# Seven quarter products instead of eight in the second products of layer 1's MLP and of the two feed-forward blocks

## The chip, the cores and the metric

The kernel runs on one core of one Trainium2 chip. Its time is the device time of one launch in microseconds (us): before the change 2538.02 us, the median of three runs (2536.36 to 2540.02). In the rows below PE is TensorE (PEld its weight loads), DVE is VectorE, ACT is ScalarE, POOL is GpSimd and SP the engine that issues most DMAs. Differences of up to 0.2% (5 us) are what a measurement of this kernel can't tell from none.

## The reference

512 tokens of width 1024 in float32 go through two layers (a short convolution, then a recurrent mixer, each with an MLP) and a block with two gated feed-forward parts around attention. Only these lines bear on the change:

```python
# layer i, width 1024 -> 4096 -> 1024
x = x + gt2[:, None, :] * (jnp.square(jax.nn.relu(h @ mlp_w1[i])) @ mlp_w2[i])
# feed-forward block, width 1024 -> 2816 -> 1024, twice
def swiglu(h, w_gate, w_up, w_down):
    return (jax.nn.silu(h @ w_gate) * (h @ w_up)) @ w_down
x = x + 0.5 * swiglu(rmsnorm(x, ffn1_norm[l]), ...)
x = x + 0.5 * swiglu(rmsnorm(x, ffn2_norm[l]), ...)
```

## The kernel before, in words

Activations lie transposed: a tile has 128 channels on the partitions and the 512 tokens along the row. A product `h @ w` is cut into blocks of 128 output channels and chunks k of 128 input channels. float32 is kept by splitting: a value is its rounded high part plus the rest, and of the four products of parts three are made. So each (block, k) costs three matmuls of 128x128 by 512 tokens: high weights by high input (line 624), high weights by low input (628), low weights by high input (630).

`PROJ` lists the products in order with the number of blocks and chunks; `pieces()` cuts their weights into pieces of up to eight 128x128 tiles (one DMA of 512 KB each into `raw_`, four buffers). Kind "m" has a piece of eight chunks of one block; kinds "e", "f" and "g" begin with 8, 6 or 4 blocks at once, chunk by chunk (so that these blocks all end within one piece), and go on as "m". For every piece ACT rounds the high part (line 1218, `WHs`, three buffers), then DVE subtracts it (line 1780, `WLs`). Both engines run through their own programs in order, and `AHEAD = 2`: in the step of piece u they first make the weights of piece u+2, and after that take what piece u has ended (`evac`). Nothing reorders this at run time. ACT can't round piece v before TensorE has used piece v-3.

In layer 1's MLP `mw1_1a` (16 blocks) and `mw1_1b` (16 blocks) are the first products. ACT takes a block out of PSUM with ReLU into `tmp` (line 1329) and writes the high part of its square to `HM` (1331), DVE squares `tmp` (1973) and writes the low part (1975). `mw2_1a` and `mw2_1b` (8 blocks of 16 chunks) read `HM`; their `evac` on DVE adds a block times its gate to X (1839). In the feed-forward blocks `f1gu` and `f2gu` (44 blocks, gate and up in turn, 22 pairs j) are the first products: DVE scales a block into one of eight buffers `pr` (2315), ACT takes the sigmoid (1588), POOL multiplies (2545), DVE makes the product h3 (2303), ACT its high part (1579), DVE the low part (2305), both in `HID`. `f1d` and `f2d` (8 blocks of 22 chunks) read `HID`. The last block of `f2d` is made in two token halves (lines 1184 to 1187), so that the last norm and the output can begin on the first half. The two products with a memory of 256 tokens (`wkv`, inputs `MNs`) already use matmuls of 256 columns at lines 624 to 630.

Of the kernel before, what the change touches and what calls it, by code (L numbers as in the profile page):

```python
# [71 lines left out]


# [74 lines left out]
class Banks:  # L148
# [204 lines left out]
def memory_order():  # L353
# [10 lines left out]
    for n in range(16):  # L364
# [8 lines left out]
            "w_o": ("back", "m", "m1"), "mw2_1a": ("m", "m2", None), "mw2_1b": ("m2", "fg", "fg"),  # L373
            "f1d": ("f1", "at", "at"), "w_out": ("at", "xa", "xa"), "wo": ("xa", "f2", "f2"),
            "f2d": ("f2", "end", "end")}
GATE = {"cw_out": (0, 2), "mw2_0a": (0, 5), "mw2_0b": (0, 5), "w_o": (1, 2), "mw2_1a": (1, 5), "mw2_1b": (1, 5),
        "f1d": 0.5, "w_out": 1.0, "wo": 1.0, "f2d": 0.5}

GAINS = {"mw2_1b": "fg1", "f1d": "mix_norm", "wo": "ffn2_norm"}


def build(nc, D, out):
    ctx = ExitStack()
    with ctx:
# [7 lines left out]
        names += ["w_lo", "v_const", "v_mod", "v_norm", "v_in", "v_evac", "v_mix", "v_scan", "v_attn"]  # L392
# [26 lines left out]
        oka = sb("oka", [128, 8])  # L419

# [16 lines left out]
        HID = at_("HID", WK + 32768, [128, 2, 22, 512], F32R)  # L437
# [48 lines left out]
        pr = [tmp_[:, i] for i in range(4)] + [T2[:, 0], T2[:, 1], GH[:, 0], GH[:, 1]]  # L486
# [51 lines left out]
        hid = lambda k: (HID[:, 0, k], HID[:, 1, k])  # L538
        xm = lambda i: (lambda k: (MX[i][0][:, k], MX[i][1][:, k]))
# [8 lines left out]
        def gate(name, m):  # L548
            g = GATE[name]
            return md(*g, m) if isinstance(g, tuple) else g  # L550

# [14 lines left out]
        def pe_program(pe, on):  # L566
# [85 lines left out]

            def turn(o, x, events, sem, cols=4):
# [31 lines left out]
            def raw(u):  # L685
                on.wait_ge(*S.at("raw", u))
                return raw_[:, u % NRAW]
# [268 lines left out]
            dense("mw1_1a", h, lambda k: ("HL", "m1", k))  # L956
            dense("mw2_1a", hm, lambda k: ("mlo", "mw1_1a", k))
            dense("mw1_1b", h, lambda k: ("HL", "m1", k))
            dense("mw2_1b", hm, lambda k: ("mlo", "mw1_1b", k))
# [21 lines left out]
            def ffn(n, tag):  # L981
                dense("f%dgu" % n, h, lambda k: ("HL", tag, k), after=norms_within if tag == "fg" else norm_within(tag))
                dense("f%dd" % n, hid, lambda k: ("hlo", n, k), part=slice(0, (None, -3)[n - 1]))
# [164 lines left out]
            def ending():  # L1148

                k0, m = [0, 8, 16], 7  # L1150
# [20 lines left out]
                for hf in range(2):  # L1171
                    o = bank("f2d", m, hf)
                    for j, (u, mms, _) in enumerate(list(steps("f2d"))[-3:]):
                        s = SLOT[u]
                        if hf == 1 and j == 1:
                            factors(0)
                        if hf == 1 and j == 2:
# [1567 lines left out]
```

## Time and profile before

| | us or share |
|---|---|
| median of 3 runs | 2538.02 |
| the profiled execution, its own time | 2542.36 |
| its span | 2540.6 |
| PE busy | 2490.3 (98%) of the span |
| DVE busy | 1329.9 (52%) |
| ACT busy | 908.6 (36%) |
| POOL busy | 201.8 (8%) |
| PE on the chain that ended last | 92% |
| mean granted clock of TensorE | 0.988 |

A matmul's duration in the profile holds its way through the array, and the next one starts before it ends; what a stream of them costs is read from start to start. A row that merges several instructions gives their number after x.

### The profile page before, as it was taken

Reading aid. Unit: us, or ns where it says so; the run is one execution under the profiler, and the core shown is the slowest. Engines: PE = TensorE matmul, PEld = TensorE weight load, DVE = VectorE, ACT = ScalarE, POOL = GpSimd, SP = SyncE. Lnnn points to the kernel's source line nnn. Section 1 sums busy time; section 2 is a strip of 40 time slices with the busy share of each in tenths; the row PEclk is TensorE's granted clock in tenths of the full one; section 3 lists DMA queues with packets and bytes.
Section 4 is the critical chain, followed back from the end, with each engine's and each line's share of the span. In section 5 each row is a group of like instructions: output and inputs, shape, how many; then the busy total and the mean of one; then the engine's idle time right before and its main releaser. Section 6 shows DMA issues by size and latency. Waiting matters only on the chain.

```text
span 2540.6 us, 39183 instructions
## 1 busy us (share of the span) xinstructions
PE 2490.3 (98%) x16966; PEld 2050.9 (81%) x16966; DVE 1329.9 (52%) x1967; ACT 908.6 (36%) x1364; POOL 201.8 (8%) x176
## 2 busy tenths in 40 slices
PE   9999999999999999999999999999999999999998
PEld 7888888876787887888888888888668987888887
DVE  7865746647845446543444544432345745444433
ACT  4224323337633233431433322322256444322221
POOL 1000000000220000000000111000221000111100
PEclk9999999999999999999999999999999999999999
DMA  8563665622210003232222332333112422322232
GB/s 341 192 197 117 200 197 185 189 86 81 85 39 4 5 29 126 82 108 99 93 100 75 108 100 95 91 97 124 64 48 76 141 79 65 114 92 99 87 100 71
DMA packets 79725, 271.86 MB, mean 107 GB/s; under 512 B 8912, under 2 KB 11216, under 8 KB 79040
## 3 DMA queue, kind: packets, MB, share of 16 engines
q1 hardware_dynamic: 67696, 224.79, 26.9%
q0 software_dynamic: 11856, 44.55, 5.5%
q8 instruction: 134, 2.20, 0.3%
q14 instruction: 39, 0.32, 0.0%
HBM read 265.11 MB, written 4.19 MB: 106 GB/s over the span
## 4 chain that ended last, share of the span: by engine, by line
PE 92%; DVE 5%; ACT 2%; issue 1%; DMA 0%; SPq 0%; DVEq 0%; ACTq 0%
PE ps L624 26%; PE ps L630 22%; PE ps L628 22%; PE ps L640 3%; PE ps L643 3%; PE ps L655 1%; DVE WLs L1780 1%; PE ps L796 1%; PE ps L809 1%; DVE ada L1796 1%; PE ps L597 1%; PE ps L822 1%; PE ps L693 1%; PE ps L1119 1%; PE ps L1133 1%
## 5 line engine op out<-in xcount | busy, mean ns | idle before, releaser
L1780 DVE TENSOR_TENSOR WLs<-raw,WHs 128x1024 fp32r<-128x1024 f32 (+2 forms) x406 | 461.4, 1137 | 419.4 <-ACT WHs L1218 418.7
L624 PE MATMUL ps<-HH,WHs 128*128 128x512 f32 x1728 | 646.6, 400 | 3.7 <-DVE Pq L2332 2.1
L1218 ACT ACTIVATE WHs<-raw 128x1024 fp32r<-128x1024 f32 (+2 forms) x424 | 416.7, 984 | 550.7 <-PE ps L630 444.7
L630 PE MATMUL ps<-HH,WLs 128*128 128x512 f32 x1406 | 548.3, 390 | 1.2 <-DVE WLs L1780 1.2
L628 PE MATMUL ps<-HL,WHs 128*128 128x512 f32 x1406 | 547.7, 390 | 0.0
L624 PEld LDWEIGHTS ps<-HH,WHs 128*128 128x128 f32 x1728 | 324.9, 189 | 76.0 <-issue 11.2
L630 PEld LDWEIGHTS ps<-HH,WLs 128*128 128x128 f32 x1406 | 263.9, 188 | 57.2 <-DVE WLs L1780 1.6
L628 PEld LDWEIGHTS ps<-HL,WHs 128*128 128x128 f32 x1406 | 264.4, 188 | 53.7 <-issue 2.2
L624 PE MATMUL ps<-HM,WHs 128*128 128x512 f32 x576 | 224.1, 389 | 0.0
L628 PE MATMUL ps<-HM,WHs 128*128 128x512 f32 x576 | 224.1, 389 | 0.0
L630 PE MATMUL ps<-HM,WLs 128*128 128x512 f32 x576 | 224.1, 389 | 0.0
L2545 POOL TENSOR_TENSOR tmp<-tmp,sqa 128x512 f32<-128x512 f32 x24 | 41.2, 1721 | 1099.0 <-ACT sqa L1588 1099.0
L630 PE MATMUL ps<-HID,WLs 128*128 128x512 f32 x330 | 128.4, 389 | 0.0
L624 PE MATMUL ps<-HID,WHs 128*128 128x512 f32 x330 | 128.4, 389 | 0.0
L628 PE MATMUL ps<-HID,WHs 128*128 128x512 f32 x330 | 128.4, 389 | 0.0
L630 PEld LDWEIGHTS ps<-HM,WLs 128*128 128x128 f32 x576 | 108.1, 188 | 22.5
L628 PEld LDWEIGHTS ps<-HM,WHs 128*128 128x128 f32 x576 | 108.1, 188 | 22.4
L624 PEld LDWEIGHTS ps<-HM,WHs 128*128 128x128 f32 x576 | 108.1, 188 | 22.4
L1796 DVE CUSTOM_DVE_ANT_0 ada<-ada,cbc 128x1024 f32<-128x1024 f32 x96 | 116.9, 1217 | 0.1
L1264 ACT ACTIVATE sqa<-X 128x512 f32<-128x512 f32 x63 | 39.8, 632 | 203.2 <-DVE X L1839 203.2
L1973 DVE TENSOR_TENSOR tmp<-tmp 128x512 f32<-128x512 f32 x64 | 44.2, 690 | 102.7 <-ACT HM L1331 102.6
L1329 ACT ACTIVATE tmp<-ps 128x512 f32<-128x512 f32 x64 | 38.0, 593 | 150.0 <-PE ps L630 150.0
(419 smaller groups left out, 3449.0 us busy)
## 6 DMA issues: line engine op xcount, KB each, us to landing
ada<-in_adaw POOLq DMA_DIRECT2D x80, 512.0 KB, 4.5
raw<-in_f1gu_m SPq DMA_DIRECT2D x38, 512.0 KB, 3.3
raw<-in_f2gu_m SPq DMA_DIRECT2D x38, 512.0 KB, 3.2
raw<-in_mw_0b SPq DMA_DIRECT2D x32, 512.0 KB, 3.5
raw<-in_mw_1b SPq DMA_DIRECT2D x32, 512.0 KB, 3.5
raw<-in_w_in_m SPq DMA_DIRECT2D x18, 512.0 KB, 3.3
ada<-in_adaw SPq DMA_DIRECT2D x16, 512.0 KB, 15.7
raw<-in_cw_in_m SPq DMA_DIRECT2D x16, 512.0 KB, 3.4
```

The costliest lines, as they stand in the source:

```text
L624: pe.matmul(o[m], WHs[:, s, w], hi, start=k == 0, stop=False)
L628: pe.matmul(o[m], WHs[:, s, w], lo, start=False, stop=False)
L630: t = pe.matmul(o[m], WLs[:, s, w], hi, start=False, stop=k == DEPTH_K[name] - 1)
L640: pe.matmul(o[m], WLs[:, s, 128 * c:128 * c + 128], x(k)[0], start=False, stop=False)
L643: t = pe.matmul(o[m], WHs[:, s, 128 * c:128 * c + 128], x(k)[1], start=False, stop=False)
L1218: act.activation(WHs[:, SLOT[v], 0:n], raw_[:, v % NRAW, 0:n], ACT.Copy).then_inc(*S.up("w_hi", ("hi", v)))
L1264: act.activation(sqt[f % 2][:, 0:n], src, ACT.Square).then_inc(*S.up("a_norm", ("sq", tag, f)))
L1329: act.activation(tmp_[:, m % 4], taken(name, m), ACT.Relu).then_inc(*S.up("a_evac", ("relu", name, m), ("free", name, m)))
L1780: dve.tensor_tensor(WLs[:, s, 0:n], raw_[:, v % NRAW, 0:n], WHs[:, s, 0:n].bitcast(F32), SUB).then_inc(*S.up("w_lo", ("lo", v)))
L1796: dve.tensor_tensor_reduce(tile, tile, cbc, 1.0, 0.0, MUL, ADD, mod[:, u:u + 1]).then_inc(*S.up("v_mod", ("dot", u)))
L1973: dve.tensor_tensor(x, x, x, MUL).then_inc(*S.up("v_evac", ("t2", name, m)))
L2545: pool.tensor_tensor(a_, a_, sqt[j % 2], MUL).then_inc(*S.up("g_ffn", ("ga", n, j)))
```

## The change

The input of a second product is grouped in pairs of chunks, its output in pairs of blocks, and the tokens in two halves (`early`, `late`). A quad of two blocks by two chunks by two halves took eight products of 128x128 by 256 tokens (in the form of four of 512); by Strassen's scheme in Winograd's form it takes seven, of sums of weight tiles and of sums of inputs. This is done for `mw2_1a` and `mw2_1b` (now 12 chunks each, `mw2_1c` takes the last 8 as before), and for the first 12 of the 22 chunks of `f1d` and `f2d` (`_a`; `_b` takes the last 10 as before). The first products are cut alike; `mw1_1a` is now 12 blocks, 8 of them at once, then 4.

```diff
-        ("mw1_1a", "e", 16, 8), ("mw2_1a", "m", 8, 16), ("mw1_1b", "m", 16, 8), ("mw2_1b", "m", 8, 16),
-        ("f1gu", "f", 44, 8), ("f1d", "m", 8, 22),
+        ("mw1_1a", "e", 12, 8), ("mw2_1a", "s", 8, 12), ("mw1_1b", "m", 12, 8), ("mw2_1b", "s", 8, 12),
+        ("mw1_1c", "m", 8, 8), ("mw2_1c", "m", 8, 8),
+        ("f1gu_a", "f", 24, 8), ("f1d_a", "s", 8, 12), ("f1gu_b", "m", 20, 8), ("f1d_b", "m", 8, 10),
...
-        ("f2gu", "f", 44, 8), ("f2d", "m", 8, 22)]
+        ("f2gu_a", "f", 24, 8), ("f2d_a", "s", 8, 12), ("f2gu_b", "m", 20, 8), ("f2d_b", "m", 8, 10)]
+BANK = [1, 2, 1, 3, 1, 2, 1]
+BEFORE = {2: 0, 4: 2, 5: 1, 6: 4}
+INPUT_GROUP = [0, 2, 1, 3, 1, 2, 3]
+SUMMED = (1, 2, 4, 6)
...
+            def fast(name):
+                src = name.replace("mw2", "mw1")
+                for a in range(BLOCKS[name] // 2):
+                    o = {}
+                    for i in range(7):
+                        u, b, g = FIRST[name] + 7 * a + i, BANK[i], INPUT_GROUP[i]
+                        if b not in o:
+                            o[b] = bank(name, a, b, hold=True)[:, 0:256]
+                        else:
+                            on.wait_ge(*S.at("drawn", name, a, BEFORE[i]))
...
+                        for k in range(n):
+                            w = slice(128 * k, 128 * k + 128)
+                            on.wait_ge(*S.at("ch", src, k, g))
+                            pe.matmul(o[b], WHs[:, s, w], HT[:, 0, k, x], start=k == 0 and i not in BEFORE, stop=False,
+                                      skip_group_check=i in BEFORE)
+                            on.wait_ge(*S.at("cl", src, k, g))
+                            pe.matmul(o[b], WHs[:, s, w], HT[:, 1, k, x], start=False, stop=False, skip_group_check=i in BEFORE)
+                            on.wait_ge(*S.at("lo", u))
+                            t = pe.matmul(o[b], WLs[:, s, w], HT[:, 0, k, x], start=False, stop=k == n - 1, skip_group_check=i in BEFORE)
...
+            def draw(name, a, i):
...
+                dve.scalar_tensor_tensor(out=x, in0=taken(name, a, b)[:, 0:256], scalar=gate(name, m) if sign > 0 else minus_gate(name, m),
+                                         in1=x, op0=MUL, op1=ADD).then_inc(*S.up("v_evac", *events))
...
+            def combinations(src, k, even, odd, t1, t2, t3, t4):
+                dve.tensor_tensor(t3, odd[:, late], even[:, late], SUB).then_inc(*S.up("v_in", ("T3", src, k)))
+                on.wait_ge(*S.at("T1", src, k))
+                dve.scalar_tensor_tensor(out=t2, in0=t1, scalar=-1.0, in1=odd[:, late], op0=MUL, op1=SUB).then_inc(*S.up("v_in", ("T2", src, k)))
+                on.wait_ge(*S.at("T2", src, k))
+                dve.scalar_tensor_tensor(out=t4, in0=t2, scalar=-1.0, in1=odd[:, early], op0=MUL, op1=SUB).then_inc(*S.up("v_in", ("T4", src, k)))
...
+            def hidden_fast(name):
+                def finish(m):
+                    k, x = m // 2, tmp_[:, m % 4]
+                    if m % 2 == 0:
+                        low(name, k, 0, x[:, early])
+                    else:
+                        low(name, k, 2, T2[:, 1])
+                        low(name, k, 1, T2[:, 0])
+                        low(name, k, 3, x)
```

`fast` is TensorE's part; `draw` (after each of the seven products), `combinations` (128x256 each) and `hidden_fast` are DVE's. The weights of one pair of output blocks come in four DMAs of 384 KB, the four quarters, each of six 128x128 tiles (768 wide); four of the seven pieces are sums of quarters, which DVE makes in `sum_quarters`, called one piece before the weights' low part. Each of the seven pieces is 6 chunks by 3 matmuls. Per pair of input blocks the input has seven 256-token groups, written as one of 256 (group 0) and three of 512 (groups 1 to 3), each with a high part by ACT (`high`, line 1466) and a low part by DVE (`low`, line 2219). The buffers `pr` go from four pairs to three, since `GH` now holds a weight sum. In `f2d_b` the last block in token halves has 10 chunks instead of 22, and the small matmuls of the last norm go in after its chunks 4 and 7 of the second half.

On DVE, in `mw1_1a`, this is what is done when the first 8 blocks have ended (tmp: the block; HM or HT: high and low parts; T_78: the input sums; WLs: low weights). Before, from the fifth of these blocks on:

```order
945 L1973 TENSOR_TENSOR tmp<-tmp 128x512
946 L1975 TENSOR_TENSOR HM<-tmp,HM 128x512
947 L1973 TENSOR_TENSOR tmp<-tmp 128x512
948 L1975 TENSOR_TENSOR HM<-tmp,HM 128x512
949 L1973 TENSOR_TENSOR tmp<-tmp 128x512
950 L1975 TENSOR_TENSOR HM<-tmp,HM 128x512
951 L1973 TENSOR_TENSOR tmp<-tmp 128x512
952 L1975 TENSOR_TENSOR HM<-tmp,HM 128x512
953 L1780 TENSOR_TENSOR WLs<-raw,WHs 128x1024
```

Now, one pair of blocks out of the four:

```order
945 L2234 TENSOR_TENSOR tmp<-tmp 128x512
946 L2219 TENSOR_TENSOR HT<-T_78,HT 128x512 x2
947 L2219 TENSOR_TENSOR HT<-tmp,HT 128x512
948 L2208 TENSOR_TENSOR T_78<-tmp 128x256
949 L2234 TENSOR_TENSOR tmp<-tmp 128x512
950 L2219 TENSOR_TENSOR HT<-tmp,HT 128x256
951 L2211 TENSOR_TENSOR T_78<-tmp 128x256
952 L2213 SCALAR_TENSOR_TENSOR T_78<-T_78,tmp 128x256
953 L2215 SCALAR_TENSOR_TENSOR T_78<-T_78,tmp 128x256
```

Two blocks took 4 instructions and take 10 now; the low weights that followed all eight blocks still follow all eight.

Where `f1gu` (now its first part, `f1gu_a`) ends and the second product begins, DVE's last pair and the next weights read like this before:

```order
1212 L2315 TENSOR_TENSOR tmp<-ps,sqa 128x512
1213 L2303 TENSOR_TENSOR tmp<-tmp 128x512
1214 L2305 TENSOR_TENSOR HID<-tmp,HID 128x512
1215 L2303 TENSOR_TENSOR tmp<-tmp 128x512
1216 L2305 TENSOR_TENSOR HID<-tmp,HID 128x512
1217 L1780 TENSOR_TENSOR WLs<-raw,WHs 128x768
```

and now (T_78 and tmp: `pr`; GH and wsum: sums of weight quarters; the last but one is the draw of the first of the seven products):

```order
1369 L2606 TENSOR_TENSOR T_78<-ps,sqa 128x512
1370 L2580 TENSOR_TENSOR tmp<-tmp 128x512
1371 L2208 TENSOR_TENSOR tmp<-tmp 128x256
1372 L2219 TENSOR_TENSOR HT<-tmp,HT 128x256
1373 L2580 TENSOR_TENSOR T_78<-T_78 128x512
1374 L2211 TENSOR_TENSOR T_78<-T_78,tmp 128x256
1375 L2213 SCALAR_TENSOR_TENSOR tmp<-tmp,T_78 128x256
1376 L2215 SCALAR_TENSOR_TENSOR T_78<-tmp,T_78 128x256
1377 L2219 TENSOR_TENSOR HT<-T_78,HT 128x512
1378 L2219 TENSOR_TENSOR HT<-tmp,HT 128x512
1379 L2219 TENSOR_TENSOR HT<-T_78,HT 128x512
1380 L1955 TENSOR_TENSOR WLs<-GH,WHs 128x768
1381 L2044 SCALAR_TENSOR_TENSOR X<-ps,X 128x256
```

The last pair's work has grown from 5 instructions to 11, and the low weights of piece 2 and the draw of product 0, which product 2 waits for, stand behind them.

## Rows read from the trace of the kernel before

**Rows 1.** The page, chain that ended last: shares of the span by engine.
```profile
PE 92%; DVE 5%; ACT 2%; issue 1%; DMA 0%; SPq 0%; DVEq 0%; ACTq 0%
```
**Rows 2.** Busy time by stretch: us, PE, PEld, DVE, ACT, POOL, granted clock, DMA.
```profile
1070.00:1375.00 305.00, 305.00 (x1347) 252.65 (x1347) 132.26 (x154) 104.11 (x137) 0.00 (x0) 1.00 0.29 96
1396.00:1723.00 327.00, 327.00 (x1444) 270.79 (x1444) 151.20 (x177) 96.34 (x121) 38.25 (x22) 1.00 0.31 98
```
**Rows 3.** Chain of waits, first steps of mw1_1a, 512 columns: start, us, what.
```profile
1029.64 1.82 PE ps L640 x8
...
1062.29 1.81 PE ps L640 x8
```
**Rows 4.** Timeline, wkv, 256 columns: start, us, engine, line, what.
```profile
2009.77 0.28 PE L630 MATMUL ps<-MNs,WLs 128*128 128x256 f32 x1
...
2013.97 0.28 PE L628 MATMUL ps<-MNs,WHs 128*128 128x256 f32 x1
```
**Rows 5.** Timeline of TensorE, first matmul of block 8 of mw1_1a.
```profile
1071.19 0.39 PE L624 MATMUL ps<-HH,WHs 128*128 128x512 f32 x1
```
**Rows 6.** Timeline of DVE, the eight blocks of mw1_1a that end together.
```profile
1068.25 0.69 DVE L1973 TENSOR_TENSOR tmp<-tmp 128x512 f32<-128x512 f32 x1
1068.98 0.69 DVE L1975 TENSOR_TENSOR HM<-tmp,HM 128x512 fp32r<-128x512 f32 x1
1069.59 0.68 DVE L1973 TENSOR_TENSOR tmp<-tmp 128x512 f32<-128x512 f32 x1
...
1078.88 1.22 DVE L1780 TENSOR_TENSOR WLs<-raw,WHs 128x1024 fp32r<-128x1024 f32 x1
```
**Rows 7.** Timeline of ACT there, the ReLU of block 9 once it has ended.
```profile
1082.27 0.60 ACT L1329 ACTIVATE tmp<-ps 128x512 f32<-128x512 f32 x1 [2.95 <-PE ps L630]
```
**Rows 8.** Groups by shape: 768-wide weights (mean ns after the bar); 256-wide (min/median/max ns).
```profile
L1780 DVE TENSOR_TENSOR WLs<-raw,WHs 128x768 fp32r<-128x768 f32 x40 | 38.3, 959 | 51.2 <-ACT WHs L1218 50.9
L1218 ACT ACTIVATE WHs<-raw 128x768 fp32r<-128x768 f32 x40 | 33.4, 835 | 37.4 <-PE ps L643 27.9 <-PE ps L630 9.5
...
L1687 ACT ACTIVATE MNs<-MEM x8: 417/418/419, 1980.3 to 1996.2; 128x256 fp32r<-128x256 f32 x8
L2430 DVE TENSOR_TENSOR MNs<-MEM,MNs x8: 424/424/426, 1980.8 to 1996.7; 128x256 fp32r<-128x256 f32 x8
```
**Rows 9.** Timelines of DVE and ACT in f1gu, one pair j.
```profile
1436.60 0.69 DVE L2315 TENSOR_TENSOR tmp<-ps,sqa 128x512 f32<-128x512 f32 x1 [3.06 <-PE ps L630]
1437.21 0.68 DVE L2303 TENSOR_TENSOR GH<-GH 128x512 f32<-128x512 f32 x1
1438.59 0.69 DVE L2305 TENSOR_TENSOR HID<-GH,HID 128x512 fp32r<-128x512 f32 x1 [0.70 <-ACT HID L1579]
...
1437.92 0.63 ACT L1579 ACTIVATE HID<-GH 128x512 fp32r<-128x512 f32 x1 [5.12 <-DVE GH L2303]
```
**Rows 10.** Ending: first half block's start (first and last start), second norm spread, DVE.
```profile
L1184 PE MATMUL ps<-HID,WHs x44: 278/283/364, 2512.7 to 2529.5; 128*128 128x256 f32 x44
...
2527.29 0.60 PE L1168 MATMUL ps<-ident,r 128*128 128x128 f32 x4
...
2531.07 0.41 DVE L2503 SCALAR_TENSOR_TENSOR X<-ps,X 128x256 f32<-128x256 f32 x1
```
**Rows 11.** The clock after gaps: timeline, chain, and stretches (clock third from the end).
```profile
1022.10 1.05 PE L588 MATMUL ps<-ones,sqa 128*128 128x1 f32 x8 [0.72 <-ACT sqa L1264]
1023.88 3.62 PE L597 MATMUL ps<-ident,r 128*128 128x128 f32 x16 [0.73 <-DVE r L1811]
...
1392.58 1.78 PE ps L597 x16
...
953.99 0.50 PE L919 MATMUL ps<-GHs,WHs 128*128 128x512 f32 x1 [1.65 <-DVE WLs L1780]
...
1023.90:1027.30 3.40, 3.40 (x16) 3.30 (x16) 0.75 (x1) 0.62 (x1) 0.00 (x0) 0.52 0.00 0
952.00:956.00 4.00, 2.35 (x49) 1.60 (x49) 1.23 (x1) 1.66 (x3) 0.00 (x0) 1.00 0.00 0
```

More of the change, by code:

```diff
@@ L70, with load_read @@
 POOLED = range(FIRST["w_in"] + 8, LAST["w_in"] + 1)
+LOADS = []
+RAW = {}
+for _u, _p in enumerate(WANT):
+    if _p[1] != "s":
+        RAW[_u] = len(LOADS)
+        LOADS.append((_u, None))
+    elif _p[3] == 0:
+        for _q in range(4):
+            RAW[_u, _q] = len(LOADS)
+            LOADS.append((_u, _q))
+HALT_LOAD = RAW[HALT]
+def load_read(load):
+    v, q = LOADS[load]
+    if q is not None:
+        return [("lo", v), ("lo", v + 4), ("lo", v + 5), ("sum", v + 6)][q]
+    return ("used" if v in WHOLE else "lo", v)
 TOKENS = [slice(0, 256), slice(256, 512)]
@@ L955, in pe_program @@
             norm("m1")
[L956 to L959, printed above, removed]
+            for part in "ab":
+                dense("mw1_1" + part, h, lambda k: ("HL", "m1", k))
+                fast("mw2_1" + part)
+            dense("mw1_1c", h, lambda k: ("HL", "m1", k))
+            if KIND["mw2_1c"] == "s":
+                fast("mw2_1c")
+            else:
+                dense("mw2_1c", hm, lambda k: ("mlo", "mw1_1c", k))
             def norm_within(tag):
@@ L1344, in within @@
                         shifted("m%d" % layer, layer, 3, i + 3)
-                for half in "ab":
-                    dense("mw1_%d%s" % (layer, half), hidden("mw1_%d%s" % (layer, half)), within if half == "a" else None)
-                    dense("mw2_%d%s" % (layer, half), residual("mw2_%d%s" % (layer, half)))
+                for part in MLP[layer]:
+                    one, two = "mw1_%d%s" % (layer, part), "mw2_%d%s" % (layer, part)
+                    dense(one, (hidden_fast if KIND[two] == "s" else hidden)(one), within if part == "a" else None)
+                    dense(two, residual(two))
             mlp(0)
@@ L1994, in within @@
                         after(i)
-                for half in "ab":
-                    dense("mw1_%d%s" % (layer, half), hidden("mw1_%d%s" % (layer, half)), within if half == "a" else after)
-                    dense("mw2_%d%s" % (layer, half), residual("mw2_%d%s" % (layer, half)), after)
+                for part in MLP[layer]:
+                    one, two = "mw1_%d%s" % (layer, part), "mw2_%d%s" % (layer, part)
+                    dense(one, (hidden_fast if KIND[two] == "s" else hidden)(one), within if part == "a" else after)
+                    dense(two, residual(two), after)
             mlp(0, ada_step)
@@ L2560, in weights @@
             def weights(first, last):
-                for v in range(first, last):
+                for r in range(first, last):
+                    v, q = LOADS[r]
                     name, kind, a, k, n = WANT[v]
```

374 lines of the change are left out of this document (283 added, 91 removed), and 3 rows, old and new, of the table RESIDUAL.

## The prediction, written before the changed kernel ran

> **What bounds the kernel now.** The chain that ended last is the first view: 92% of it is TensorE [rows 1]. The second is busy time by stretch: from 1070 to 1375 us (layer 1's MLP) and from 1396 to 1723 us (first feed-forward block) TensorE is busy in every microsecond at full clock, while DVE has work for 132 of 305 and 151 of 327 us [rows 2]. So the kernel is a stream of matmuls, and the change has to be judged by the length of that stream and by new gaps in it. The third view is the timeline, read from start to start. At 512 columns 18 groups of 8 matmuls take 1062.29 - 1029.64 = 32.65 us, or 0.2267 us each [rows 3]. At 256 columns 35 steps take 2013.97 - 2009.77 = 4.20 us, or 0.120 us each [rows 4]. Half the columns cost 53% of the time, not 50%.
>
> **The stream.** A product cut to 12 chunks was 8 x 12 x 3 = 288 matmuls of 512 columns, 65.3 us. As quads it is 4 x 7 x 6 x 3 = 504 matmuls of 256 columns, 60.5 us. One eighth of the arithmetic (8.2 us) shrinks to 4.8 us. Four products give 19.2 us. The ending takes part of this back and gives another part. Before, its last block in halves began at 2512.7 and the second norm spread at 2527.29, 14.6 us later; the last X update waits for the outputs of the first half and starts 3.8 us after the spread [rows 10], and that part stays. Now the first half has 30 matmuls (3.6 us), the second 24 up to the spread (2.9 us), and the small norm matmuls about 0.7: 7.2 us. The whole of f2d was 7 x 66 x 0.2267 + 14.6 = 119.3 us up to the spread and is now 60.5 + 7 x 30 x 0.2267 + 7.2 = 115.3. So f2d gives 4.0 us instead of 4.8, and all four give 3 x 4.8 + 4.0 = **18.5 us** (rounded).
>
> The Trainium skill, page "TensorE: Matmul & The Clock Gate", section "Back-to-back issue gap", gives a fixed cost of only 2.5 ns beside the columns. By it a matmul would take 109 ns at 256 columns and 216 ns at 512, and an estimate from that page alone is a gain of 28 us. The rows have 120 and 227 ns for this kernel's operands, so they decide, and the page's rule gets no chance of its own.
>
> **Inside a quad nothing new should wait.** A piece of weights now lasts 18 x 0.120 = 2.16 us on TensorE. DVE gives each piece one 768-wide low part (0.96 us, and about 0.88 to the next start, since starts lie 0.08 closer than durations: 0.61 for 0.69 in [rows 6]), one draw of 256 from PSUM (0.41 [rows 10]), and for four of seven a 768-wide sum (0.88). That is at most 2.2 us in four steps and 1.3 in three, 12.6 us of the quad's 15.1. ACT gives 0.84 [rows 8]. The low part of piece u+2 is wanted two pieces later, so a step that is 0.05 late shows nowhere. Cost taken: 0. If the cover is gone, it would cost what DVE exceeds 15.1 us by, sixteen times.
>
> **The burst in mw1_1a.** Eight blocks end together. DVE took 16 instructions for them, from 1068.25 to 1078.88, and then made the low weights of block 10 [rows 6]. Block 8 starts at 1071.19 [rows 5], blocks last 24 x 0.2267 = 5.44, so block 10 starts at 1082.07 and wants its low weights at 1082.5, with 2.4 us to spare. Now each pair of blocks costs DVE: two squares (0.61 each), a 256-wide low part (0.42 by [rows 8], 0.34 to the next), T1, T3, T2, T4 (0.34, 0.34, then 0.46 where the next waits for it, 0.34), three 512-wide low parts (0.61 each), and 0.2 of waiting for ACT's first high part. That is 5.1 us; the first pair lacks the low parts before it. 1.1 + 2.1 + 3 x 5.1 = 18.4, so the low weights of block 10 start at 1086.7 and are there at 1087.95. TensorE waits **5.4 us**, in two parts (ACT's high part is late too, at about 1085.5). The three-operand 256-wide forms on SBUF are not in the trace; between the 0.34 taken and the 0.69 of a 512-wide one this wait is 4 to 9 us; I take the form of equal width. Queued behind it: the low weights of block 11 and the work of blocks 8 and 9, which still end before block 11 starts.
>
> **The four entries to a quad product.** Before, a second product wanted its last input only at chunk 15 or 21, over 10 us after it began. Now piece 0 reads all six chunk pairs in 2.2 us, piece 1 another group of each, and piece 2 waits for its weights and for the draw of product 0, which both stand behind the last input pair in DVE's order. With T the end of the last block, for mw1_1b: ReLU T+0.20 to 0.80 [rows 7], square to 1.55, low part of group 0 at 1.5, T3, T2, T4 done 3.05, high part of group 2 by ACT to 3.75 and of groups 1 and 3 to 4.85, high weights of piece 2 to 5.6, low weights 5.65 to 6.6, draw to 6.95. Piece 2 starts at T+7.05 instead of 4.32: **2.7 us**. In mw1_1a DVE comes late from the burst, with two blocks' work and two weight sums in 10 us: by the same steps 3.7 us. In the feed-forward blocks the chain is scale, h3 of pair 10, h3 of pair 11 (0.61 to 0.71 apart [rows 9]), then as above: T4 is done at T+4.25, the low weights at 7.9, the draw at 8.35, and piece 2 starts at 8.45: 4.1 us each, 8.2 for two. Sum of the entries **14.7 us**, the largest wait in each being some 2.4 us ahead of piece 2. The bursts of six blocks at the start of f1gu_a and f2gu_a gain four 256-wide steps and two more low parts, some 3 us of DVE; the low weights behind them have two blocks (10.9 us) of room, as in mw1_1a, with 6 blocks instead of 8 in front. I take 0.3 us each (0 to 3). New waits together: 5.4 + 14.7 + 0.6 = **20.7 us**. Gates, buffers (three pairs of `pr` where j lasts 10.9 us and its work about 5) and DMAs (4 of 384 KB in 15.1 us) come at nothing: the matmuls hide them.
>
> **The clock.** Two gaps of 0.72 and 0.73 us with little work between them were followed by a stretch at a granted clock of 0.52, in which 16 transposes took 3.62 us instead of 1.78 [rows 11], so 1.7 us was lost. A lone gap of 1.65 us left the clock at 1.00 [rows 11]. The burst (over 5 us idle with a few matmuls in it) and the two feed-forward entries (some 3.7 us idle in 5) should each bring such a fall; the two MLP entries (2.4 us in one piece) are open. Cost 3 x 1.7 = **5.1 us**, from 0 to 5 x 1.84 = 9.2.
>
> **The sum.** -18.5 + 20.7 + 5.1 = +7.3 us on the profiled execution (own time 2542.36, span 2540.6). That execution was 4.3 us over the median of the runs; the difference is taken over to the median: 2538.0 + 7.3 = **2545.3 us**. Its own range, from the bounds above, is 2540 to 2553.
>
> **The rivals.**
> - *The clock holds.* Against it stand the double gap of [rows 11], for it the lone gap. Then -18.5 + 20.7 = +2.2: 2540 us, no change that can be told.
> - *The entries are shorter than drawn*, so the change is faster. The place is piece 2 of the first quad of each product, the price the 2.4 us before it, four times. It decides once all new waits are below 13.4 us (18.5 less the 0.2% of a measurement). That needs ACT's high parts and DVE's low parts to overlap better than one after another in queue order: if each entry is 2 us shorter (the last input's three low parts no longer in front) and the burst 3.4 us, with one fall of the clock, it is -18.5 + 20.7 - 8 - 3.4 + 1.7 = -7.5: 2530.5 us. For it speaks that DVE is idle over half of these stretches [rows 2]; against it that the order is fixed and the idle time lies after, not before, the low weights.
> - *DVE becomes the bound inside the quads.* For it: four steps of seven hold 2.2 us of work against 2.16. Against: the quad has 2.5 us to spare. If each piece ran 0.15 us over (a wait for the previous result before each draw would do it), 112 pieces give 16.8 us: 2562 us.
> - *The seven products aren't cheaper at all*: it would need 0.13 us per matmul. The rows of 256 columns, with the same three forms and new weights for each matmul, exclude it, unless the column sums read worse; within the third rival.
>
> **Chances.** Forecast 0.50, clock holds 0.20, shorter entries 0.18, DVE as bound 0.12. Faster by over 0.2% (5 us, what a measurement of this kernel can tell; under 2532.9): the third case and a sliver of the second, 0.19. Within 0.2%: most of the case with the clock held and a sixth of the forecast, 0.25. Slower (over 2543.1): 0.56. The range that holds 8 of 10 is 2530 to 2557.
>
> **What would show it.** Matmuls of 256 columns 0.120 us apart inside quads, and no waits there: the stream is right. In mw1_1a a wait of 5 us for ACT's and DVE's weights ahead of block 10: the burst. Ahead of piece 2 of four products a gap of 2.4 us that ends with a draw, and 1 us before it for a low input part: the entries. A granted clock below 1 after the burst and in both feed-forward entries: the fall. The forecast is wrong if the waits of TensorE grow by less than 13 us, or if gaps recur in each quad.

## The result and the profile after

The changed kernel takes 2545.39 us (median of 14 runs, 2542.5 to 2549.83), the kernel before beside it 2537.94 (14 runs, 2535.47 to 2542.18). The ratio is 1.0027 with a 95% interval of 1.0019 to 1.0036: the change costs 7 us, or 4.8 to 9.1 us by the interval. Forecast were 2545.3 us.

The page of the changed kernel has these totals, its chain by engine and its quad matmuls (busy us, mean ns; idle before them and who ended it):

```profile
PE 2474.5 (97%) x17794; PEld 2073.4 (82%) x17794; DVE 1528.2 (60%) x2352; ACT 973.3 (38%) x1484; POOL 199.2 (8%) x176
PE 88%; DVE 6%; ACT 2%; issue 2%; SPq 1%; DMA 1%; POOL 0%; DVEq 0%; ACTq 0%
L758 PE MATMUL ps<-HT,WHs 128*128 128x256 f32 x672 | 192.3, 286 | 8.3 <-DVE X L2044 7.7
```

TensorE is busy 15.8 us less than before (2490.3) and waits more: its share of the chain falls from 92% [rows 1] to 88%, DVE's rises from 5% to 6%. The third line is new: 7.7 us of TensorE's waiting ends with a draw. The same two stretches as in [rows 2] (us, PE, PEld, DVE, ACT, POOL, granted clock, DMA):

```profile
1070.00:1375.00 305.00, 296.20 (x1757) 264.73 (x1756) 222.20 (x329) 132.33 (x191) 0.00 (x0) 0.98 0.29 94
1396.00:1723.00 327.00, 324.07 (x1661) 277.64 (x1660) 198.32 (x270) 111.00 (x150) 37.02 (x22) 1.00 0.30 95
```

Before, TensorE had no idle microsecond in either; now 8.8 and 2.9 us are idle, and in the first the clock isn't full. The view of waits between 1020 and 1400 us (total, times, longest) gives the releasers:

```profile
PE ps L758 <- DVE X L2044: 3.9, 2, 2.0
PE ps L713 <- ACT WHs L1348: 2.7, 1, 2.7
PE ps L719 <- DVE WLs L1955: 2.0, 1, 2.0
```

Stage by stage, from one first matmul to the next in the two traces, in us:

| stage | before | after | difference |
|---|---|---|---|
| layer 1's MLP (before from 1027.55, after from 1024.51) | 348.29 | 353.96 | +5.7 |
| first feed-forward block | 365.2 | 363.3 | -1.9 |
| what lies between | 424.8 | 424.7 | -0.1 |
| second feed-forward block to the end of the span | 374.7 | 377.0 | +2.3 |
| from mw1_1a's start to the end | 1513.0 | 1519.1 | +6.0 |

Ahead of mw1_1a, where nothing was changed, the profiled execution of the changed kernel happened to be 3.0 us shorter. So the two spans (2540.6 and 2543.6) differ by 3.0 only; the 1513.0 and 1519.1 us are the fair comparison, and their difference lies within the interval of the ratio.

### The profile page after: what moved, and what is told of

It is laid out like the page before. It is cut to its first block, busy times and chain, and to the rows that moved or that the text cites. A ratio compares the mean times of both kernels' runs of the same rounds, so it can differ in the third digit from the quotient of the medians.

```text
span 2543.6 us, 41536 instructions
## 1 busy us (share of the span) xinstructions
PE 2474.5 (97%) x17794; PEld 2073.4 (82%) x17794; DVE 1528.2 (60%) x2352; ACT 973.3 (38%) x1484; POOL 199.2 (8%) x176
## 4 chain that ended last, share of the span: by engine, by line
PE 88%; DVE 6%; ACT 2%; issue 2%; SPq 1%; DMA 1%; POOL 0%; DVEq 0%; ACTq 0%
PE ps L713 22%; PE ps L719 18%; PE ps L717 18%; PE ps L729 4%; PE ps L732 4%; PE ps L758 3%; PE ps L763 3%; PE ps L761 3%; PE ps L770 1%; DVE WLs L1955 1%; PE ps L911 1%; PE ps L924 1%; ACT WHs L1348 1%; SPq L2874 1%; DVE HT L2219 1%
## 5 line engine op out<-in xcount | busy, mean ns | idle before, releaser
L1955 DVE TENSOR_TENSOR WLs<-raw,WHs 128x1024 fp32r<-128x1024 f32 (+3 forms) x430 | 465.6, 1083 | 283.0 <-ACT WHs L1348 281.5
L1348 ACT ACTIVATE WHs<-raw 128x1024 fp32r<-128x1024 f32 (+3 forms) x448 | 421.6, 943 | 454.8 <-PE ps L719 259.6
L758 PE MATMUL ps<-HT,WHs 128*128 128x256 f32 x672 | 192.3, 286 | 8.3 <-DVE X L2044 7.7
L761 PE MATMUL ps<-HT,WHs 128*128 128x256 f32 x672 | 192.4, 286 | 1.0 <-DVE HT L2219 0.7
L763 PE MATMUL ps<-HT,WLs 128*128 128x256 f32 x672 | 191.6, 285 | 0.0
L713 PE MATMUL ps<-HM,WHs 128*128 128x512 f32 x384 | 149.4, 389 | 0.0
L717 PE MATMUL ps<-HM,WHs 128*128 128x512 f32 x384 | 149.4, 389 | 0.0
L719 PE MATMUL ps<-HM,WLs 128*128 128x512 f32 x384 | 149.4, 389 | 0.0
L758 PEld LDWEIGHTS ps<-HT,WHs 128*128 128x128 f32 x672 | 130.4, 194 | 10.0 <-DVE X L2044 8.6
L761 PEld LDWEIGHTS ps<-HT,WHs 128*128 128x128 f32 x672 | 130.3, 194 | 2.5 <-DVE HT L2219 2.2
L763 PEld LDWEIGHTS ps<-HT,WLs 128*128 128x128 f32 x672 | 130.4, 194 | 0.0
L2606 DVE TENSOR_TENSOR tmp<-ps,sqa 128x512 f32<-128x512 f32 x60 | 40.8, 689 | 105.5 <-PE ps L719 105.5
L713 PEld LDWEIGHTS ps<-HM,WHs 128*128 128x128 f32 x384 | 72.1, 188 | 15.1
```

Of the source, the lines that this page charges most:

```text
L713: pe.matmul(o[m], WHs[:, s, w], hi, start=k == 0, stop=False)
L717: pe.matmul(o[m], WHs[:, s, w], lo, start=False, stop=False)
L719: t = pe.matmul(o[m], WLs[:, s, w], hi, start=False, stop=k == DEPTH_K[name] - 1)
L758: pe.matmul(o[b], WHs[:, s, w], HT[:, 0, k, x], start=k == 0 and i not in BEFORE, stop=False, skip_group_check=i in BEFORE)
L761: pe.matmul(o[b], WHs[:, s, w], HT[:, 1, k, x], start=False, stop=False, skip_group_check=i in BEFORE)
L763: t = pe.matmul(o[b], WLs[:, s, w], HT[:, 0, k, x], start=False, stop=k == n - 1, skip_group_check=i in BEFORE)
```

## The experiments

The theory: the stream of matmuls did get 18.5 us shorter; three kinds of loss took it back and more, namely the burst in mw1_1a, the wait for a draw at each entry, and falls of TensorE's clock after these gaps. Rivals: the burst or the entries cost little; the clock isn't a cost of its own; the 256-column matmuls or DVE inside the quads ate the gain. Each ratio is to the kernel before on the same chip, so ratios can be set side by side and medians of different chips can't: the kernel before took 2537.2 us beside e1 to e4, 2540.13 beside e5 to e8 and 2538.75 beside e9 and e10. e8 rests on two runs, e4 on four, e10 on six, the others on ten or more. "From mw1_1a" is the time from its first matmul to the end of the span in the profiled execution (before 1513.0).

| kernel | median us | ratio, 95% interval | from mw1_1a |
|---|---|---|---|
| changed (first) | 2545.39 | 1.0027, 1.0019 to 1.0036 | 1519.1 |
| e1_four | 2537.2 | 0.9997, 0.9988 to 1.0006 | 1512.3 |
| e2_entry | 2536.88 | 1.0, 0.9991 to 1.0009 | 1513.7 |
| e3_both | 2531.57 | 0.9977, 0.9968 to 0.9986 | 1506.2 |
| e4_narrow | 2560.97 | 1.0091, 1.0077 to 1.0105 | 1534.4 |
| e5_fill | 2538.99 | 0.999, 0.998 to 1.0 | 1508.2 |
| e6_end | 2533.69 | 0.9971, 0.996 to 0.9982 | 1504.8 |
| e7_slack256 | 2548.95 | 1.0031, 1.002 to 1.0041 | 1519.3 |
| e8_slack512 | 2563.26 | 1.0086, 1.006 to 1.0112 | 1531.6 |
| e9_fill_all | 2541.0 | 1.001, 1.0001 to 1.0019 | 1514.0 |
| e10_again | 2546.92 | 1.0035, 1.0023 to 1.0048 | 1519.6 |

### e1_four: four blocks at once in mw1_1a instead of eight

```diff
-        ("mw1_1a", "e", 12, 8),
+        ("mw1_1a", "g", 12, 8),
```

> One edit to the changed kernel: mw1_1a begins with 4 blocks at once instead of 8. Theory (the new waits are queue order on VectorE and ScalarE): behind 4 blocks VectorE has two pairs, 1.1 + 2.1 + 5.1 = 8.3 us, instead of 18.4; counted from the last chunk's start the low weights of block 10's counterpart are there after 2.5 + 8.3 + 1.2 = 12.0 us and wanted after 2.7 + 10.9 + 0.45 = 14.05, so both waits in mw1_1a (2.7 and 2.0 us in the changed kernel) vanish and with them the 6.8 us at half clock behind them (3.4 us lost). The time falls by 8 us to 2537.5, and the entry to mw2_1a loses up to 1 us more. It would fall less if at the start of mw1_1a the four-block steps (2.7 us each) outrun the inputs (up to 3 us given back). Rival (the loss of the changed kernel sits inside the quads or in the matmul stream, and the burst's wait is only moved on to the next step): the time stays within 2 us of 2545.

Measured 0.9997, 7.6 us under the changed kernel by the ratios. mw1_1a lasts 65.8 us instead of 73.8. The waits between 1020 and 1400 us are now:

```profile
PE ps L758 <- DVE X L2044: 3.9, 2, 2.0
PE ps L686 <- DVE r L2010: 0.7, 1, 0.7
```

Both waits of the burst are gone, the entries' stay (the 0.7 us lie ahead of mw1_1a and are in the changed kernel too). What it doesn't give back whole is the clock: full at the entries of mw2_1a and f1d_a in the changed kernel, it now falls there and no longer at f2d_a, one fall more in all. At mw2_1a:

```profile
1097.20:1100.40 3.20, 3.20 (x15) 3.20 (x16) 2.92 (x4) 0.85 (x1) 0.00 (x0) 0.50 0.00 0
```

### e2_entry: another order at the entries

After the last input pair DVE does the draw of product 0 and the low weights of piece 2 before the last two low parts, and ACT the high weights of piece 2 before the last two high parts. On DVE:

```diff
                 for u, _, ended in list(steps(name))[part]:
+                    if rest:
+                        evac(ended.pop())
                     ahead(u, limit)
+                    while rest:
+                        rest.pop(0)()
...
-                        low(name, k, 1, T2[:, 0])
-                        low(name, k, 3, x)
+                        others = [lambda: low(name, k, 1, T2[:, 0]), lambda: low(name, k, 3, x)]
+                        if m == BLOCKS[name] - 1:
+                            rest.extend(others)
```

> The changed kernel with another order at the entry of each quad product: after the last input pair's group 2, VectorE makes the draw of product 0 and the low weights of piece 2, then the low parts of groups 1 and 3; ScalarE makes the high weights of piece 2 before the high parts of groups 1 and 3. Nothing is added or left out. Theory (piece 2 waits for what stands behind the last inputs): low part of group 2 done at T+4.5, draw 4.4 to 4.8, low weights 4.8 to 5.7; piece 2 starts at T+4.9 and waits about 0.7 at its third matmul, so that each entry is 1.5 us shorter, 6 us in all, and one or two of the three stretches at half clock at entries may go (1.7 each). The time falls to 2536 to 2540. Rival (the gap ahead of piece 2 is set by something that the order doesn't move, a sum, a DMA, or the matmuls' own way to PSUM): within 1.5 us of 2545.

Measured 1.0. The wait for the draw is gone; a wait for low weights, of 0.5 us at most, comes twice at each entry, eight times over the run. Between 1020 and 1400 us (the last line lies ahead of mw1_1a):

```profile
PE ps L713 <- ACT WHs L1349: 2.7, 1, 2.7
PE ps L763 <- DVE WLs L1967: 1.8, 4, 0.5
PE ps L719 <- DVE WLs L1967: 1.5, 1, 1.5
PE ps L713 <- ACT HH L1422: 0.9, 1, 0.9
```

The entered products last 62.49 (MLP) and 63.70 us (feed-forward), against 63.15 and 64.35 in the changed kernel where its clock held. So the order saves only 0.66 us of waiting at each entry, where 1.5 was expected; it breaks one gap of 2.0 us into gaps of at most 0.5, and with these the clock falls at none of the four entries. From mw1_1a it gives 5.4 us: 2.6 of waiting at the entries, 3.0 of clock there and 1.4 in mw1_1a, less 1.6 for a fall at the start of f1gu_a (1377.9 us) that the changed kernel's trace doesn't have. The time came out in the expected range because the clock gave what the waits didn't.

### e3_both: both edits

> Both edits: 4 blocks at once in mw1_1a, and the new order at the entries. Theory: the two are independent, -8 and -6 and what the clock gives back, so 2530 to 2533, under the kernel before (2538) by 5 to 8 us. Rival (they share one slack, or the stream's own gain of 18.5 us isn't there): 2537 or more, not under the kernel before.

Measured 0.9977: 5.8 us faster than the kernel before and 12.7 us faster than the changed one (each by ratio). Its first stretch and the whole from mw1_1a to just before the end:

```profile
1070.00:1375.00 305.00, 303.03 (x1816) 271.01 (x1815) 215.42 (x315) 128.98 (x183) 0.00 (x0) 1.00 0.29 97
1025.00:2519.00 1494.00, 1482.53 (x7812) 1252.86 (x7810) 882.15 (x1371) 584.11 (x902) 122.20 (x66) 1.00 0.28 93
```

TensorE idles 2.0 us in the first, not 8.8, and the clock is full through both.

### e4_narrow: what narrow matmuls cost by themselves

The kernel before, each 512-column matmul of mw2_1a, mw2_1b, f1d and f2d cut in two of 256 columns, so the weights are loaded twice (what these second products then hold is not the reference's, for a reason that no run isolates; the number of matmuls and what they wait for are as described).

```diff
-                        pe.matmul(o[m], WHs[:, s, w], hi, start=k == 0, stop=False)
...
+                            for c0 in (0, 256):
+                                q = slice(c0, c0 + 256)
+                                pe.matmul(o[m][:, q], WHs[:, s, w], hi[:, q], start=k == 0, stop=False, skip_group_check=True)
...
```

> The kernel before, in which the second products mw2_1a, mw2_1b, f1d and seven blocks of f2d do each matmul of 512 columns as two of 256, with the same numbers: 1758 matmuls become 3516. Theory (a matmul costs 0.120 us at 256 columns and 0.2267 at 512, 13 ns beside the columns): +1758 x 0.0133 = +23.4 us, 2561.4. Rival 1 (only a few ns beside the columns, as with the 2.5 ns of the Trainium skill's page TensorE: Matmul & The Clock Gate, section Back-to-back issue gap): +4.4 us, 2542.4. Rival 2 (weight loads, 0.19 us long in the profile, bound a narrow stream): +1758 x (2 x 0.19 - 0.227) = +270 us.

Measured 1.0091: 23.1 us more by the ratio. The start-to-start time is 0.120 us again:

```profile
1129.84 0.28 PE L628 MATMUL ps<-HM,WHs 128*128 128x256 f32 x1
...
1131.88 0.28 PE L632 MATMUL ps<-HM,WLs 128*128 128x256 f32 x1
```

17 steps take 2.04 us. Two halves cost 0.240 us where one whole costs 0.2267: 0.013 us for each matmul added. The fixed cost of a matmul is real, and small enough for seven products to pay.

### e5_fill: the gaps filled

e1_four with seven small matmuls of ones ahead of piece 2 in each entry; the real waits stay.

```diff
+                            if a == 0 and i == 2:
+                                idle = bank("idle", name)
+                                for _ in range(7):
+                                    pe.matmul(idle[:, 0:128], ones[:, :], ones[:, :], start=True, stop=True)
```

> The kernel with 4 blocks at once in mw1_1a, and at each of the four entries TensorE does seven small matmuls on a spare bank (128 columns, about 0.22 us each, 1.6 us in all) while it would wait 1.9 us for the draw of product 0. They change no result and should fit in the wait. Theory (a gap at an entry costs twice, the wait itself and the stretch at half clock after it, 1.7 us): the waits for data stay, the three stretches at half clock behind the entries (1097, 1227 and 1517 us in that kernel's trace) vanish, and the time falls from 2537.2 by 3 to 5 us to 2532 to 2534. Rival (the half clock there is a mark in the records that costs nothing, or it comes from elsewhere): within 1 us of 2537.2, or above it by what the small matmuls overrun.

Inconclusive by the medians: 0.999 with an interval that overlaps e1's 0.9997, a gain of 1.8 us and not 3 to 5. In its trace no fall begins between mw1_1a's start and the ending; the first quads last 17.80, 17.80, 18.99 and 18.99 us against 19.19, 19.13, 20.49 and 19.00 in e1, 4.2 us less, and "from mw1_1a" is 4.1 us shorter. The two ran on different chips, so a direct test was made on one chip (e9 and e10).

### e9_fill_all and e10_again: the changed kernel with and without fillers, side by side

e9 is the changed kernel with fillers at the entries as in e5 and in both waits of the burst; e10 is the changed kernel unaltered.

```diff
+                    late = name == "mw1_1a" and mms[0][0] == 10
+                    if late:
+                        idle = bank("idle", name)
...
+                        for _ in range(10):
+                            pe.matmul(idle[:, 0:128], ones[:, :], ones[:, :], start=True, stop=True)
                     on.wait_ge(*S.at("hi", u))
...
+                        if late and i == 0:
+                            for _ in range(7):
+                                pe.matmul(idle[:, 0:128], ones[:, :], ones[:, :], start=True, stop=True)
                         on.wait_ge(*S.at("lo", u))
```

> The changed kernel as it is, with small matmuls of ones (128x128 by 128, results unused) in the gaps: 10 before block 10 of mw1_1a while it waits for its high weights, 7 before its first low weights, 7 ahead of piece 2 in each of the four entries. All waits stay. Theory (the falls of the clock are a cost of their own beside the waits; the trace of the change has a burst fall of 6.8 us at half clock and two of 3.4 us at entries): the waits remain, the three falls go, the stretch from the start of mw1_1a to the end of the span shortens by 5 to 7 us from 1519.1 us to 1512 to 1514, and the median ratio to the kernel before goes from 1.0027 to 1.0000 to 1.0008. Rival (the clock is not what costs, or the filling delays the real matmuls by as much as it saves): ratio stays at 1.002 to 1.003.

> The changed kernel unaltered, on the chip on which the filled one runs, so that the two can be compared directly. Both theories: ratio to the kernel before 1.002 to 1.0035. In its trace the falls of the clock at the entries may lie elsewhere than in the first one (which had them in mw2_1b and f2d_a); the burst's fall is expected in each.

Measured 2541.0 against 2546.92 us, ratios 1.0001 to 1.0019 against 1.0023 to 1.0048: 5.9 us by the medians, 5.6 by the traces. Timeline of e9 at the burst (the fillers are L711 and L726):

```profile
1080.64 2.39 PE L711 MATMUL ps<-ones 128*128 128x128 f32 x20
1083.50 0.50 PE L719 MATMUL ps<-HH,WHs 128*128 128x512 f32 x1 [0.47 <-ACT WHs L1362]
1084.08 1.72 PE L726 MATMUL ps<-ones 128*128 128x128 f32 x14
1086.19 0.50 PE L728 MATMUL ps<-HH,WLs 128*128 128x512 f32 x1 [0.39 <-DVE WLs L1969]
```

Each real matmul still waits for the same input, but the clock holds. Around the burst, in e9 and then in the changed kernel:

```profile
1078.00:1092.00 14.00, 13.14 (x75) 11.19 (x74) 13.80 (x27) 8.82 (x16) 0.00 (x0) 1.00 0.17 49
```

```profile
1078.00:1092.00 14.00, 9.34 (x29) 6.82 (x29) 13.80 (x27) 8.03 (x14) 0.00 (x0) 0.76 0.18 57
```

DVE does the same 27 instructions in both; the clock is 1.00 in one and 0.76 in the other. So the falls are a cost of their own beside the waits, and keeping TensorE at work in the gaps prevents them. By stage, e9 against e10: mw1_1a is 2.7 us shorter (71.54 against 74.26), mw2_1b and f2d_a 1.5 us each, the ending 0.5, and mw2_1a is 0.6 longer, since TensorE now reaches it earlier and waits there for a low input part. The ratio of 1.001 is a little above the 1.0000 to 1.0008 expected.

### e7_slack256 and e8_slack512: how much room DVE has in a quad

One more DVE addition after each draw, 256 or 512 wide, result unused.

```diff
+                dve.tensor_tensor(acc[:, 0:256], rstd[:, 0:256], rstd[:, 0:256], ADD).then_inc(*S.up("v_evac", ("spare", spare)))
```

> The changed kernel (2545.4) with one more VectorE instruction after each of the 112 draws, 256 wide, 0.34 us to the next start, on a buffer that nobody reads. Theory (inside a quad VectorE has 12.6 of 15.1 us of work): 2.4 us per quad fits in the 2.5 that are spare, so 2545 to 2549. Rival (VectorE is already the bound inside the quads, so that the quads run at its pace): +2.4 x 16 = +38 us, 2583.

> As the run before, with 512 wide instructions, 0.61 us to the next start. Theory: 12.6 + 4.3 = 16.9 us of work per quad against 15.1, so each quad is 1.8 us longer: +28 us, 2573. Rival (VectorE already the bound): +4.3 x 16 = +68 us, 2614. Second rival (VectorE has far more room than 2.5 us, since starts overlap more than read): below +10 us.

e7: 1.0031, not to be told from the changed kernel's 1.0027, and 1519.3 us from mw1_1a against 1519.1. e8: 1.0086, some 15 us more by the ratio, 12.5 by the traces. Thirty microseconds within mw2_1a (about two quads) of the changed kernel, e7 and e8:

```profile
1116.00:1146.00 30.00, 30.00 (x253) 30.00 (x252) 25.70 (x37) 11.86 (x14) 0.00 (x0) 1.00 0.31 104
```

```profile
1118.00:1148.00 30.00, 30.00 (x252) 30.00 (x251) 29.95 (x52) 11.85 (x14) 0.00 (x0) 1.00 0.34 106
```

```profile
1118.00:1148.00 30.00, 29.60 (x236) 28.44 (x236) 30.00 (x47) 10.91 (x13) 0.00 (x0) 1.00 0.30 93
```

DVE goes from 25.7 to 29.95 us of 30, and TensorE does as many matmuls as before. Only at 30.00 does it lose, 236 matmuls for 252. The third and fourth quads of the MLP's products then last 16.5 us each, those of the feed-forward blocks 15.9 and 16.1, instead of 15.1. I had expected 28 us for e8, counting every quad at the full excess. The first quad doesn't lengthen (its entry wait covers the extra work), the second by 0 to 0.5 us, and the draw in the feed-forward blocks takes 0.42 us and not 0.49, so the excess is smaller there. That is 10 us in all; falls at all four entries instead of two add 3.0, and small differences elsewhere make it 12.5.

### e6_end: the last X update ahead of most outputs

e3_both, and in the ending the last X update goes after three of the first half's eight outputs instead of after all eight.

```diff
-            for hf in range(2):
+            last_draw(0)
+            for hf in range(2):
...
+                    if (hf, f) == (0, 2):
+                        last_draw(1)
```

> The kernel with both edits, and at the end VectorE makes the last X update of the second token half after three of the eight outputs of the first half instead of after all eight. Theory (the shorter last block gave nothing past the point where the update stands behind the outputs, so TensorE's wait for its square grew from 1.6 to 3.0 us): the update comes 1.9 us earlier and so does the end: 2531.6 - 1.9 = 2529.7. Rival (the end is set by the last outputs and their stores, whatever the update does): 2531.6.

Measured 0.9971 (0.996 to 0.9982). DVE's timeline of the ending:

```profile
2517.79 1.26 DVE L2832 SCALAR_TENSOR_TENSOR OUT<-X,vec,ps 128x256 f32<-128x256 f32 x3 [1.16 <-PE ps L1292]
2518.97 0.42 DVE L2821 SCALAR_TENSOR_TENSOR X<-ps,X 128x256 f32<-128x256 f32 x1
2519.30 2.04 DVE L2832 SCALAR_TENSOR_TENSOR OUT<-X,vec,ps 128x256 f32<-128x256 f32 x5
```

From f2d_b's start to the end it takes 66.4 us against 68.7 in e3, 2.3 less where 1.9 was expected. The ratios 0.9971 and 0.9977 overlap; that this edit gains is seen in the trace alone. Against the kernel before the gain is 7.4 us by the ratio and 8.2 from mw1_1a. By ratio and from mw1_1a it is the fastest version run; its median is above e3's, but so is that of the kernel before beside it (2540.13 against 2537.2).

## Why the prediction was right

It was right in its mechanism: a stream that gets shorter, new waits at the burst and the entries, and falls of the clock behind them. Its terms were near. That 2545.3 and 2545.39 us agree to 0.1 us is luck: the two traces differ by 6.0 us and not by 7.3, single terms are off by up to 1.6 us with both signs, and the interval alone leaves 4.8 to 9.1 us. The range of 2540 to 2553 us given "from the bounds above" isn't their sum either, which reaches from 2538 to 2555 or more. The terms below are what the trace of the changed kernel shows between mw1_1a and the end.

- **The stream, -18.5 us forecast, -18.3 measured.** Inside the quads matmuls start 0.120 us apart; on the timeline of TensorE 35 steps take 4.20 us, as in [rows 4]:

```profile
1112.49 0.28 PE L758 MATMUL ps<-HT,WHs 128*128 128x256 f32 x1
...
1116.69 0.28 PE L763 MATMUL ps<-HT,WLs 128*128 128x256 f32 x1
```

  Full quads last 15.12 us, so a product without its entry is 60.5, as forecast. f2d: taking its entry's excess (65.85 - 60.48) off, it is 115.4 us up to the spread, forecast 115.3, against 119.3 before. The last X update stays where it was relative to the spread, 3.79 us after it [rows 10], because the eight outputs are still in front:

```profile
2530.16 0.60 PE L1292 MATMUL ps<-ident,r 128*128 128x128 f32 x4
```

```profile
2530.81 3.22 DVE L2804 SCALAR_TENSOR_TENSOR OUT<-X,vec,ps 128x256 f32<-128x256 f32 x8 [1.16 <-PE ps L1292]
2533.95 0.41 DVE L2797 SCALAR_TENSOR_TENSOR X<-ps,X 128x256 f32<-128x256 f32 x1
```

  By the gap for isolated matmuls on the page "TensorE: Matmul & The Clock Gate" of the Trainium skill, section "Back-to-back issue gap", with its 2.5 ns of fixed cost, an estimate of this term would be 28 us. The 1758 matmuls that e4_narrow adds cost 23 us, 0.013 each; by the page they would be an estimate of 4.4 us. The measurement decides.

- **Inside a quad, 0 forecast.** No wait recurs in them. DVE is busy 25.7 of 30 us, 12.9 a quad where 12.6 was worked out, and e7 and e8 put the limit where the sum had it, at about 15 us a quad.

- **The burst, +5.4 forecast, 5.0 measured.** DVE's 18.4 us were 18.1 (1065.82 to 1083.93); a pair of blocks costs 5.0 where 5.1 was forecast. So the 256-wide forms on SBUF do cost what forms of that width cost elsewhere (0.42 us, 0.34 to the next start). On the timeline (PE and DVE rows of the burst):

```profile
1079.42 0.39 PE L719 MATMUL ps<-HH,WLs 128*128 128x512 f32 x1
1082.51 0.50 PE L713 MATMUL ps<-HH,WHs 128*128 128x512 f32 x1 [2.70 <-ACT WHs L1348]
1082.85 0.40 PE L717 MATMUL ps<-HL,WHs 128*128 128x512 f32 x1
1083.14 0.42 DVE L2213 SCALAR_TENSOR_TENSOR T<-T,tmp 128x256 f32<-128x256 f32 x1
1083.93 1.22 DVE L1955 TENSOR_TENSOR WLs<-raw,WHs 128x1024 fp32r<-128x1024 f32 x1
1085.21 0.79 PE L719 MATMUL ps<-HH,WLs 128*128 128x512 f32 x1 [1.96 <-DVE WLs L1955]
```

  The waits of 2.7 and 2.0 us in brackets are idle time. From start to start the loss is 3.09 + 2.36 us less two steps of 0.2267, that is 5.0 us, and that is what the other terms are measured by. The forecast's times were those of the trace before, in which mw1_1a begins 3.04 us later (1027.55 against 1024.51). In the changed kernel's time it had ACT's high part at about 1082.5, where block 10 does begin, and the low weights at 1084.9, where they are there at 1085.15. TensorE came to block 10 some 0.65 us late (see the clock), so its wait is shorter than 5.4.

- **The entries, +14.7 forecast, 13.1 measured.** Where the clock held they cost 2.7 us in the MLP and 3.9 us in the feed-forward blocks (63.15 and 64.35 less 60.48), forecast 2.7, 3.7, 4.1 and 4.1. The step that was off is mw2_1a's 3.7: DVE had caught up in the 10 us between the burst and the entry, and TensorE idles 1.97 us ahead of piece 2 in both entries of the MLP. In e9, where TensorE arrives 2.7 us sooner after the burst, this entry does become 0.6 us longer, so the forecast's reason was sound and its size wasn't. The gap ends as forecast with the draw. The waits ahead of it are 0.45 us from start to start in the MLP, less than the 1 us named, and 1.7 us in the feed-forward blocks, more than that. In the timeline of mw2_1a:

```profile
1103.81 0.95 DVE L1955 TENSOR_TENSOR WLs<-GH,WHs 128x768 fp32r<-128x768 f32 x1
1104.67 0.48 DVE L2044 SCALAR_TENSOR_TENSOR X<-ps,mod,X 128x256 f32<-128x256 f32 x1
...
1105.21 0.38 PE L758 MATMUL ps<-HT,WHs 128*128 128x256 f32 x1 [1.97 <-DVE X L2044]
```

- **The starts of f1gu_a and f2gu_a, +0.6 forecast, 1.3 measured.** f2gu in both parts is 242.81 us against 242.13, and f1gu as much longer once the fall of the clock that the kernel before had there is taken out. The estimate of 0.3 us each was half of the 0.7 measured, within its bounds of 0 to 3.

- **The clock, +5.1 forecast, 4.8 measured.** It is made up otherwise than forecast. The fall after the burst lasts 6.8 us, twice as long as the others; TensorE is busy for 5.39 of them at half clock, so 2.7 us are lost (e9's mw1_1a is shorter than e10's by the same 2.7). Of the two feed-forward entries only the second falls, and of the two MLP entries, left open, the second does (1.5 us each, from the first quads of 19.29 and 20.49 against 17.79 and 18.99). The three stretches:

```profile
1083.80:1090.60 6.80, 5.39 (x13) 4.23 (x14) 6.80 (x12) 4.14 (x7) 0.00 (x0) 0.50 0.26 75
...
1233.80:1237.20 3.40, 3.40 (x18) 3.40 (x19) 2.79 (x4) 0.84 (x1) 0.00 (x0) 0.53 0.00 0
...
2309.20:2312.60 3.40, 3.40 (x18) 3.40 (x17) 2.50 (x5) 0.97 (x2) 0.00 (x0) 0.50 0.04 7
```

  And the kernel before had a fall at f1gu's start that the prediction didn't see: its row of full clock ([rows 2]) begins at 1396 us, after it. It is absent in both profiled executions of the changed kernel, which gives 1.6 us back:

```profile
1382.40:1385.80 3.40, 3.40 (x11) 2.72 (x11) 0.75 (x5) 2.52 (x4) 0.00 (x0) 0.50 0.14 54
```

  Whether that is the change's doing is open: e4_narrow, made from the kernel before, has no fall there, and e2, e6 and e8, made from the changed one, have it. Last, the fall ahead of mw1_1a, in code that is the same in both kernels, reaches 1.3 us into mw1_1a in the changed kernel's trace and ends before it in the other, which by half of 1.3 costs this comparison an estimate of 0.65 us:

```profile
1024.50:1025.80 1.30, 1.29 (x3) 1.11 (x4) 1.30 (x2) 0.60 (x1) 0.00 (x0) 0.50 0.00 0
```

  2.7 + 1.5 + 1.5 - 1.6 + 0.65 = 4.75. Of this the two last terms may belong to the two executions and not to the change. Removing the falls at the burst and the entries of the changed kernel gained 5.9 us by the medians (e9 against e10).

The sum of the measured terms is -18.3 + 5.0 + 13.1 + 1.3 + 4.8 = +5.9 us, against +6.0 between the traces and about +7 between the medians.

Of the rivals, "the clock holds" fell by e9. "The entries are shorter" was wrong for the change as it stands, but named the remedy: with the last low parts taken out of the way (e2) and the burst out (e1) the result is 2531.57 us (e3), close to the 2530.5 given for it. It was reached in another way than that rival said. The entries shrank by 0.66 us each, not 2; the rest was the clock and the whole burst. "DVE becomes the bound" is excluded by e7, which fills DVE to 29.95 of 30 us at no cost. "Not cheaper at all" is excluded by the cadence and by e4.

What isn't settled is why, of four entries with gaps of nearly the same length, just these fall.

## What to carry to other kernels

A change that takes arithmetic off the bounding engine has to be summed with what it puts at the seams: here 19 us of new waits and 5 us of clock stood against 18.3 us, and nothing inside the steady stream. Where the saved work is an eighth, look first at how many inputs end at once (half the burst removed the whole wait) and at what stands in queue order in front of the first thing that the bounding engine needs. And judge a reordering by the length of the largest gap, not by the sum of waits alone: with 0.66 us less waiting per entry, and the rest in pieces of 0.5 us, the clock fell at none of the twelve entries in the traces of e2, e3 and e6, where the undivided gaps of the changed kernel (first and e10), e1, e7 and e8 brought 13 falls at 20 entries. That the division and not the smaller sum did it is argued, not shown; e5 and e9, which fill the gap and keep the wait, have no fall at their eight entries either.

## What the runs showed of the hardware that was not expected

- Gaps of 2.0 us, each with a shorter one before it, were followed by a stretch of 3.4 us at 1.2 GHz (granted clock 0.5) at some entries and not at others, repeatably: in three profiled executions (the changed kernel's first, e10 and e7) there are falls at mw2_1b and f2d_a and none at mw2_1a and f1d_a. With the burst gone (e1) they were at mw2_1a, mw2_1b and f1d_a and not at f2d_a. So where a fall comes depends on more than the gap itself.
- The first part of the kernel, the same code in all, ended between 1020.50 (e2) and 1030.58 us (e5) in twelve profiled executions, with 31 to 48 us of it at half clock. A comparison of single spans carries this 10 us of noise. A comparison from a common point in the code doesn't: for the unaltered changed kernel 1519.1 and 1519.6. What it can still carry is a fall that begins ahead of the point and reaches past it, by up to 1.9 us in these traces (e9, e10), or one that comes in one execution and not in another.
- DVE at 29.95 of 30 us, in order and with dependences on two other engines, cost the stream inside the quads nothing measurable (e7): full quads last 15.12 us, as without the added work.
